# Two-layer GLA and pooling decoder step on 8 cores: another model of engines and transfers, other step lists, and another order of the first loads

## What is computed

```python
xn = rmsnorm(h, norm_g)
z = xn @ w_in                                                # (B,L,IN_COLS)
q, k, v, ga, u, gb, alow, mg = jnp.split(z, IN_OFFSETS, axis=-1)
la = jax.nn.log_sigmoid(alow @ w_alpha + b_alpha) / GATE_TAU
...
b = jnp.cumsum(la, axis=2)                                   # per chunk of 64
o = einsum(A, v) + einsum(q * exp(b), S)                     # A: decayed, causal q.k
S_new = exp(b_last) * S + einsum(k * exp(b_last - b), v)
...
ya = (rms(o) * gla_gain * silu(ga)) @ w_a
yb = (pool_mix(u) * silu(gb)) @ w_b
h = h + (s_a * ya + s_b * yb) @ w_out                        # s: merge gates
```

## Time and profile before

| | us |
|---|---|
| median of three runs | 1164.29 (1163.81 to 1164.81) |
| profiled execution | 1169.49 |
| its span on core 7, the slowest, by the profile | 1167.9 |
| spans of the eight cores | 1157.5 to 1167.9 |
| PE busy | 1125.2 (96%) |
| DVE, POOL, ACT busy | 619.8, 600.6, 514.6 |
| DMA queues' share of the 16 DMA engines | SP 42.0%, POOL 20.5% |

### The profile page before, as it was taken

One profiled execution on the slowest core, in us unless ns is written; L12 is line 12 of the kernel. 1 busy time (PEld: TensorE's weight loads), 2 busy tenths in 40 slices (PEclk: granted clock), 3 DMA queues, 4 the chain that ended last, 5 costly groups with the idle time before them and its releaser, 6 DMA issues.

```text
span 1167.9 us, 27837 instructions; the slowest of 8 cores (1157.5 to 1167.9 us)
## 1 busy us (share of the span) xinstructions
PE 1125.2 (96%) x10110; PEld 879.9 (75%) x10110; DVE 619.8 (53%) x923; ACT 514.6 (44%) x1044; POOL 600.6 (51%) x909
## 2 busy tenths in 40 slices
PE   7999999999999999999999999999999999999997
PEld 3777677777787777787767787776778877878874
DVE  4466687665633543444435656766755244434433
ACT  3636457566433333332345545555444233333333
POOL 4187788876933332333434866858676332223232
PEclk9999999999999999999999999999999999999998
DMA  9955458574688998996687234434467765565321
GB/s 195 196 123 127 118 105 159 133 154 85 143 190 189 256 248 254 230 250 171 172 157 165 56 91 78 97 80 84 97 119 186 151 225 205 184 218 190 110 88 47
DMA packets 129242, 178.84 MB, mean 153 GB/s; under 512 B 82064, under 2 KB 90640, under 8 KB 129104
## 3 DMA queue, kind: packets, MB, share of 16 engines
q1 hardware_dynamic: 113840, 141.01, 42.0%
q0 software_dynamic: 15264, 36.05, 20.5%
HBM read 139.85 MB, written 54.59 MB: 166 GB/s over the span
## 4 chain that ended last, share of the span: by engine, by line
PE 69%; DMA 12%; issue 6%; POOL 6%; DVE 4%; ACT 3%; SPq 0%; POOLq 0%; DVEq 0%; ACTq 0%
PE psum L525 69%; DMA arena<-w 5%; DMA arena<-arena 4%; POOL arena L567 4%; ACT arena L552 3%; DVE arena L579 2%; DMA arena<-sgla 2%; POOL arena L574 1%; POOL arena L599 1%; DMA arena<-hin 1%; DVE arena L567 1%; DVE arena L770 1%; DMA XN<-arena 0%; ACT L552 0%; SPq L599 0%
## 5 line engine op out<-in xcount | busy, mean ns | idle before, releaser
L525 PE MATMUL psum<-arena 128*128 128x256 bf16 (+8 forms) x10006 | 1121.5, 276 | 34.2 <-DVE arena L579 10.3
L525 PEld LDWEIGHTS psum<-arena 128*128 128x128 bf16 (+3 forms) x10006 | 874.0, 98 | 276.9 <-DVE arena L579 15.4
L567 POOL TENSOR_TENSOR arena<-arena 128x256 bf16<-128x256 f32 (+13 forms) x347 | 344.2, 997 | 262.5 <-DVE arena L579 204.2
L579 DVE SCALAR_TENSOR_TENSOR arena<-arena,psum 128x256 f32<-128x256 f32 (+7 forms) x474 | 269.8, 601 | 279.2 <-PE psum L525 208.7
L574 POOL TENSOR_SCALAR arena<-arena 128x256 bf16<-128x256 f32 (+7 forms) x396 | 182.7, 471 | 214.3 <-ACT arena L552 142.3
L552 ACT ACTIVATE arena<-psum,arena 128x256 f32<-128x256 f32 (+4 forms) x428 | 172.0, 456 | 264.4 <-PE psum L525 203.0
L552 ACT ACTIVATE arena<-psum 128x256 bf16<-128x256 f32 (+6 forms) x260 | 161.2, 631 | 188.8 <-PE psum L525 165.3
L552 ACT ACTIVATE arena<-arena 128x1024 bf16<-128x1024 f32 (+4 forms) x140 | 141.3, 1016 | 176.3 <-DVE arena L579 90.9
L579 DVE SCALAR_TENSOR_TENSOR arena<-psum,arena 128x256 bf16<-128x256 f32 (+6 forms) x125 | 91.1, 760 | 113.0 <-PE psum L525 107.5
L579 DVE SCALAR_TENSOR_TENSOR arena<-arena 128x256 bf16<-128x256 f32 (+4 forms) x124 | 129.4, 1057 | 40.0 <-POOL arena L567 35.4
L599 POOL DMA_DIRECT2D arena<-w x106 | 62.1, 595 | 49.4 <-POOL arena L567 12.1
(11 more groups left out here) (9 smaller groups left out, 10.4 us busy)
## 6 DMA issues: line engine op xcount, KB each, us to landing
arena<-hin SPq DMA_DIRECT2D x32, 512.0 KB, 5.8
arena<-sgla SPq DMA_DIRECT2D x32, 512.0 KB, 5.6
nsg_s<-arena SPq DMA_DIRECT2D x32, 512.0 KB, 5.7
arena<-w POOLq DMA_DIRECT2D x30, 512.0 KB, 15.8
arena<-w POOLq DMA_DIRECT2D x48, 224.0 KB, 4.6
arena<-XN SPq DMA_DIRECT2D x20, 512.0 KB, 5.6
H<-arena SPq DMA_DIRECT2D x16, 512.0 KB, 4.6
arena<-H SPq DMA_DIRECT2D x16, 512.0 KB, 4.9
```

Source lines behind the costliest of these rows:

```text
L525: return S.add("pe", lambda e: e.matmul(out, lhsT=lhsT, rhs=rhs, start=start, stop=stop, skip_group_check=sgc), r=[lhsT, rhs], w=[out], co ...
L567: return S.add(eng, lambda e: e.tensor_tensor(out=out, in0=in0, in1=in1, op=op), r=[in0, in1], w=[out], cost=c)
L579: return S.add("dve", lambda e: e.scalar_tensor_tensor(out=out, in0=in0, scalar=scalar, in1=in1, op0=op0, op1=op1), r=r, w=[out], cost=eco ...
```

## The change

It replaces the planner's model. For all engines but PE an operation holds its engine for less than its cost (95, 80 and 20 ns less on ACT, DVE and POOL) and its result is usable later (260, 220, 190 ns; PE 350). Operations of DVE that read two SBUF operands, and all of POOL's, hold a common lock in the model, one at a time. All transfers, from both queues, go through one server in the order of their issue, with issue costs of 430 ns (1300 ns for transposes) on SP and 600 ns on POOL. The four `stt` of a pair's pooling windows now depend on the last window add (`after=[w_]`). Both step lists are replaced. In the start `cols` goes ahead of `cf`, `walpha` ahead of tile 2, tile 2 waits until tile 0 has landed, tile 3 until tile 1 has, tile 16 until tile 2 has. The pieces of w1 become 17 steps P among the other steps, each free to go when tile 0 has landed. The cast of `walpha`, `colsh` and `nba` become a step WL.

```diff
...
+        if eng != "pe" and not dma:
+            cost, lat = max(40.0, cost - self.OVERLAP[eng]), self.LAT[eng]
         self.ops.append(dict(eng=eng, fn=fn, deps=deps, dma=dma, token=None, cost=float(cost), lat=float(lat),
-                             attach=attach, fine=fine))
+                             attach=attach, fine=fine, lock=not dma and (lock or eng == "pool")))
...
+    OVERLAP = dict(act=95.0, dve=80.0, pool=20.0)
+    LAT = dict(act=260.0, dve=220.0, pool=190.0)
...
+                if ops[idx]["lock"]:
+                    st_ = max(st_, lock + (60.0 if e == "dve" else 0.0))
...
             if op["dma"]:
-                issue = 60.0 if e == "sp" else 900.0
+                issue = 600.0 if e == "pool" else 1300.0 if op["fine"] else 430.0
                 free_t[e] = st_ + issue
-                begin = max(st_ + issue + (1500.0 if e == "pool" else 0.0), dma_free[e])
-                both = max(0.0, dma_free[other[e]] - begin)
-                r = 1.85 if e == "sp" else 0.54
-                dma_free[e] = begin + op["cost"] + min(both, 20000.0 if op["fine"] else r * op["cost"])
-                dma_free[other[e]] += min(op["cost"], both / r)
-                done_t[idx] = dma_free[e] + 2000.0
+                dma_free = max(st_ + issue + (1500.0 if e == "pool" else 0.0), dma_free) + op["cost"]
+                done_t[idx] = dma_free + 2000.0
             else:
                 free_t[e] = st_ + op["cost"]
                 done_t[idx] = st_ + op["cost"] + op["lat"]
+                if op["lock"]:
+                    lock = free_t[e]
...
-            if f == 1.0 and not psum_:
-                return 260.0 + ptr + 1.12 * n_
             return 130.0 + ptr + 1.06 * n_ * (1.0 if psum_ else f)
...
         x0_ = dma(hb[0], rows_of(hin, 0))
+        dma(cols, cols_d[:, :])
         dma(cft, cf_d[:, :])
-        dma(hb[1], rows_of(hin, 1))
-        dma(cols, cols_d[:, :])
-        for t in range(2):
-            x3_ = dma(hx[t], rows_of(hin, 2 + t))
-        dma(hm[0:NM, :], rows_of(hin, 16))
+        x1_ = dma(hb[1], rows_of(hin, 1))
+        dma(Tst[:, 0:512], walpha_d[0])
+        x2_ = dma(hx[0], rows_of(hin, 2), after=[x0_])
+        dma(hx[1], rows_of(hin, 3), after=[x1_])
+        dma(hm[0:NM, :], rows_of(hin, 16), after=[x2_])
...
                 windows(ue, a3, b3, 271)
+                w_ = len(S.ops) - 1
                 for g in range(4):
                     src = a3[:, g] if g % 2 == 0 else b3[:, g - 1]
-                    stt(z3[:, g, :], src[:, 15:271], 1.0 / WINDOWS[g], ue[:, g, 15:271], ALU.mult, ALU.subtract)
+                    stt(z3[:, g, :], src[:, 15:271], 1.0 / WINDOWS[g], ue[:, g, 15:271], ALU.mult, ALU.subtract, [w_])
...
         STEPS = [
-            ("F/0 V1b/0 V0a/0:2 V1a/0:1 UM F/1 F/8 D/8:01 V1b/1 K/8:1 D/0 D/1 V1a/1:2 V0b/0 Q/8 X/2 Q/0 V0a/1 Q/1 "
-             "GF V0/8 KT/8 MS/8 U/8 K/1:2 GA0/8 K/0 GA0/0:2 SC0/8 V0b/1 SC1/0:1 GA1/1:2 SC0/0 GB/8 KT/0 PY/8:2 "
...
+            ("F/0 P WL P F/1 P V0a/0:2 P F/8 P V1b/0 P P V1b/1 P P P P V1a/0:1 D/8:22 UM P K/8:1 D/0 D/1:02 P "
+             "V1a/1:2 X/2 P V0a/1 P V0/8 KT/8 GF Q/0 Q/8 P Q/1 P MS/8:1 U/8 K/1 GA0/8:2 K/0 GA1/1 SC1/0 V0b/0 "
...
         def phase1(l):
             walf = Tst[:, 0:512]
-            dma(walf, walpha_d[l])
-            cp("dve", wal, walf)
-            for r in (32, 96):
-                tt("dve", wal[r:r + 32, :], walf[r:r + 32, :], wal[r:r + 32, :], ALU.subtract)
+            if l:
+                dma(walf, walpha_d[l])
+
+            def alpha(p):
+                if l == 0:
+                    ts("dve", colsh, cols, 0.5)
...
+                cp("dve", wal, walf)
...
+            def first(p):
+                d_, s_ = w1q.pop(0)
+                dma(d_, s_, eng="pool", after=[x0_], rate=310.0)
...
-            if l == 0:
-                for i, (d_, s_) in enumerate(queue):
-                    dma(d_, s_, eng="pool", after=[x0_ if i < 3 else x3_], rate=310.0)
-                queue.clear()
...
```

More of the change, by code:

```diff
@@ L552, in act, with both @@
             return S.add("act", lambda e: e.activation(out=out, in_=in_, func=func, **kw), r=r, w=w, cost=c)
+        def both(*aps):
+            return all(a.tensor.name == "arena" for a in aps)
         def ecost(eng, n_, f, aps):
@@ L574, in ts, with stt @@
             return S.add(eng, lambda e: e.tensor_scalar(out=out, in0=in0, **kw), r=r, w=[out],
-                         cost=ecost(eng, fsz(out), 0.55, [out] + r))
-        def stt(out, in0, scalar, in1, op0, op1):
+                         cost=ecost(eng, fsz(out), 0.55, [out] + r), lock=both(in0, out))
+        def stt(out, in0, scalar, in1, op0, op1, after=()):
             r = [in0, in1] + ([] if isinstance(scalar, float) else [scalar])
@@ L580, in stt @@
                                                                  op1=op1), r=r, w=[out],
-                         cost=ecost("dve", fsz(out), 1.0, [out] + r))
+                         cost=ecost("dve", fsz(out), 1.0, [out] + r), lock=both(in0, in1), after=after)
         def cp(eng, out, in_):
@@ L639, in build_nc @@
         cp("dve", lo_f, cft[:, CF_LO:CF_LO + 1])
-        ts("dve", colsh, cols, 0.5)
-        for l_ in range(NL):
-            ts("dve", nba[:, 4 * l_:4 * l_ + 4], cols[:, l_ * NCL + CL_BA:l_ * NCL + CL_BA + 4], -1.0)
         memset("dve", nhalf, -0.5)
```

28 lines of the change are left out of this document (18 added, 10 removed), and 44 rows, old and new, of the table STEPS.

## The result

The changed kernel takes 1182.91 us (median; 1181.27 to 1185.11) against 1164.55 (1163.81 to 1165.77) of the kernel before on the same chip: a ratio of 1.0158, 95% interval 1.0138 to 1.0178. On another chip it was 1.0137 (1.0114 to 1.0160). Forecast were 1157.3 and a range up to 1169.5: wrong in sign and outside the range. The profiled execution took 1181.27.

A forecast was written before the change was run, and what follows sets the result against it. PE was taken as the bound, busy 1125.2 of 1167.9 us, so only its idle time could move; -1.5 + 0.5 - 6 + 0 = -7.0 us took the profiled 1169.5 to 1162.5, the median to 1157.3, range 1148.5 to 1169.5.

The forecast's parts named there:

- Term 1: First loads at the start: tile 16 moves behind the first V pieces, weights come earlier; -1.5 us, ends -4.2 and +1.5.
- bytes can only change places: Step for the first loads: the DMA share shows nothing idle there, so only tile 16's 1.5 us of transfer counts.
- 16.5 named as the sign: Sign at the start that the forecast is right: PE begins its V work at about 16.5 us, against 18.14 before.
- Rival 1: Slower: from 45 to 75 us weights land later than planned, PE stands up to 4.8 us longer; median 1168, chance 0.24.
- Term 2: End of the weights: last piece still lands at about 72.8 us, an earlier PE waits longer; +0.5 us, ends 0 and +4.8.
- Term 3: Pooling windows in both phases 1: `stt` after the last add free DVE; -6 of 8.1 us idle, ends 0 and -8.1.
- the mean under 700 ns: Sign for the pooling windows: the mean of the 64 window `stt` on DVE falls from 974 ns to under 700.
- DVE sits there: Step for the pooling windows: DVE sits in a window `stt` ahead of PE's four longest phase 1 idle times, 8.1 us.
- Term 4: All other order: remaining 14.6 us of PE's idle time in the two phases 1; 0, ends -4 and +4 us.
- its code is not changed: 0: Step for phase 2: 2.0 us of idle time in layer 0, code not changed, so an effect of 0.
- Rival 2: No change: window `stt` after the last add is blocked by POOL's next operations; sum -1, 1163.3 us, chance 0.14.
- Rival 3: More gain: half of the other idle time goes as well, together -15 us, 1149.5 us, chance 0.12.

The follow-up runs named there:

- e4_before_w: Kernel before, old model and lists, planned anew with only the four window `stt` made dependent on the last window add: 1.0053 of the kernel before.
- e7_short_adds: Kernel before, order kept, POOL's four window adds cut to 16 positions, so z is not right: 0.9906 of the kernel before.
- e9_adds_dve: Kernel before, order kept, the prompt pairs' window adds run on DVE instead of POOL: 0.9951 of the kernel before.
- e3_w2_earlier: Changed kernel, order kept but five phase 2 weight pieces issued earlier, and pieces of steps W without pacing waits: 1.0061 of the kernel before.
- e11_new_lists: Changed kernel without the token-load waits, transfer costs fitted to the traces, both step lists reworked: 1.0131 of the kernel before.
- e12_new_lists_dve: Changed kernel without token-load waits, fitted transfer costs, window adds on DVE in the planner too, lists reworked for that: 0.9969 of the kernel before.
- e10_after_all: Changed kernel's order with five weight pieces earlier and two meant to be held for O, plus window adds moved to DVE: 1.0085 of the kernel before.

## Why the prediction was wrong, step by step

- **Term 1** (-1.5, at worst +1.5): measured +10.8 us at 41.7. The step that failed is "bytes can only change places", with which the loads were costed as landings alone. They are also what the plan is made from. The prediction had the fact in hand: the earlier trace rows show SP overtaking POOL, so the planner has tile 16 some 10 us later (33.3) than the chip (22.6), and the steps that need it take a late place in PE's fixed stream. It was used for the weights only. Planned without the gates, the lag is 1.2; with the gates gone on the chip alone, 14.1. PE's V work did begin earlier, at 17.28 (18.14 in the earlier trace rows, 16.5 named as the sign).
- **Rival 1** had the sign, and a part of the transfers: the first seven pieces are later than planned by 1.9 to 4.9 us, the third lands at 21.8, as it estimated for the kernel before. Its place is wrong. From the eighth piece on the landings are within 1.2 us of the plan (the last 68.0 and 68.1), and from 60 to 75 us PE has no idle time at all; the landing at 72.8 was carried over from the kernel before and did not hold. What it missed is what SP's early landings do to the order. The Trainium skill, "DMA: Bandwidth & Descriptors", section "Queues, rings and completion order", lets an engine go round the queues packet by packet. Tile 16 at 22.6 instead of 33.3 agrees, and so do the late first seven pieces.
- **Term 2** (+0.5): the waits of the earlier trace rows, 1.68 and 0.75 us, are gone, and the idle time from 60 to 75 us with them, 2.9. But PE is 7 us late there (lag 7.3 at 79.3), so it is a gain in name only.
- **Term 3** (-6): of its signs, the mean under 700 ns came with 564. Two others did not: an idle time of 2.22 us still ends with DVE behind a window, and the idle time from 600 to 900 us is 11.1, not about 6. In the body of layer 1's phase 1 the lag falls by 5.1 us, near the size forecast; whether the freed DVE is the reason is not shown, since the dependence under the old lists, planned anew, gives nothing (`e4_before_w`). The failed step is the one from "DVE sits there" to "PE gets that time": the four `stt` were thought free once moved, and at pair 7 they are blocked by the next POOL operations. The Trainium skill, "SBUF — State Buffer", section "SBUF: two separate sides", has the shared port pair held for one instruction; the one `stt` of 4.81 us lay beside two of POOL's, 4.23 us in all, so here too the block outlasts one. `e7_short_adds` and `e9_adds_dve` make it likely that the sum also lacked POOL's own time; no run isolates it.
- **Term 4** (0, at most +4): measured +11 us between 297 and 358, on all cores, and +4 from 868 to 900 on two, the slowest among them. The failed step is "its code is not changed: 0" for phase 2. The steps W and L stand in the lists of phase 1, and the new list left 37 us without a piece. Each W should have been followed to its use in C/5. With five pieces earlier 6.5 of the 11 us come back, the pacing waits being gone as well (`e3_w2_earlier`). This one place is larger than the whole range given to order.
- **Rival 2** happened at one place, 2.22 us. **Rival 3** did not.

The lag is 15.2 us at 900 and 11.8 in the spans: between 1100 and 1150 us core 7 of the kernel before loses 2.8 us that its other cores do not, at a granted clock of 0.90 in its last stage. Not settled: the 5 us at the entry of layer 1 (idle time from 600 to 660 is 3.5 against 2.2 us, the rest not placed); O's wait; and what the start is worth at the end, since the changed order with its start alone replaced was not run (the lag is 7.3 at 79.3 and 2.4 at 128.7).

## What to carry to other kernels

Where a planner fixes the streams, a change of its model is a change of the order: ask of every load that the model lands late which steps it pushes back, and of every transfer of a moved step who uses it, in the next phase too. A model that is nearer to the trace in many costs can still give a slower kernel, because each in-order stream passes one late transfer on to all behind it; a wait that only spaces out transfers can do the same there (`e11_new_lists`). When an engine blocks another, try to take the work off the blocking engine, with the order kept. The two kernels here that compute everything and were faster than the kernel before, `e9_adds_dve` (0.9951) and `e12_new_lists_dve` (0.9969), both have the window adds on DVE; on the changed order the same move gained nothing (`e10_after_all`).

## What the runs showed of the hardware

Transfers of two queues do not go in the order of their issue: tile 16's load on SP, issued at 12.7 behind seven weight pieces on POOL's queue, landed at 22.6, where first come would have said 33.3. The first seven pieces landed 1.9 to 4.9 us later than first come, all others within 1.2 us of it. The 512 KB write and read of O took 6.1 and 7.7 us on the slowest core of the changed kernel and 4.4 and 4.9 on that of the kernel before; over all cores the ranges overlap (5.0 to 7.0 and 4.5 to 8.3 against 4.4 to 7.7 and 3.5 to 6.1), and what weight pieces beside them cost was not isolated. The same transfer can differ much between cores: one weight piece of `e9_adds_dve` took 22.2 us on core 4 and 9.8 to 13.5 on the others. A DVE `stt` with both operands in SBUF can be held over several POOL operations: 7.23 us in a stretch of five, 4.81 beside two of 4.23 in all. And the granted clock fell to the 1.2 GHz level (0.50) behind stops of PE of 3.4 to 5.1 us, for instance from 37 to 43 us; in the whole kernel the same matmuls took 3.3 us more of PE's busy time.
